# Expert stage of a two-layer decoder trunk: products of three token pairs staggered in one step, outputs brought back in 64-row products, pair-wise weights

## The reference, cut to what matters

```
g_idx = argmax(t @ w_group + b_group)              # 4 groups of experts
top_p, top_i = top_k(softmax(e_logits[g_idx]), 2)   # 2 of the 8 experts of that group
weights = g_w * top_p / sum(top_p)
y_e = (silu(x_e @ w_gate[e]) * (x_e @ w_up[e])) @ w_down[e]   # 1024 -> 256 -> 1024, for each expert e
out[token] = x[token] + sum over its 2 experts of weight * y_e
```

## Time and profile before

| | |
|---|---|
| median of 3 runs | 1148.37 us (1148.35 to 1148.47) |
| the profiled execution | 1148.85 us |
| its span, first to last instruction | 1147.0 us |
| TensorE busy | 1103.0 us, 96% |
| VectorE busy | 672.4 us, 59% |
| ScalarE busy | 372.9 us, 33% |
| GpSimd busy | 67.5 us, 6% |
| DMA queue of SyncE | 240.78 MB, 52.6% of 16 engines' span |
| mean granted TensorE clock | 0.987 |

### The profile page before, as it was taken

The page is one execution under the profiler, slowest core; times in us unless marked ns, Lnnn a source line. Parts: engine busy times, 40 slices in busy tenths (PEclk is TensorE's granted clock), DMA queues, the critical chain, the costliest instruction groups (busy, mean ns, idle before and its releaser), DMA issues.

```text
span 1147.0 us, 16734 instructions
## 1 busy us (share of the span) xinstructions
PE 1103.0 (96%) x4876; PEld 600.0 (52%) x4876; DVE 672.4 (59%) x1580; ACT 372.9 (33%) x811; POOL 67.5 (6%) x123
## 2 busy tenths in 40 slices
PE   7999999999799999999999999999997999999997
PEld 4854555556574444444457545555566544444443
DVE  4236765467685555555652477655667755555554
ACT  5226331114433333333252263210243433333332
POOL 1000000000007000000000000000000250000001
PEclk9999999999889999999999999999997999999999
DMA  9031024500319999999641300245005299999992
GB/s 351 2 109 39 1 74 147 220 1 1 151 73 406 417 421 421 423 422 422 263 157 44 103 1 1 75 147 220 1 2 220 108 404 422 421 423 422 421 422 105
DMA packets 50925, 243.20 MB, mean 212 GB/s; under 512 B 6512, under 2 KB 16784, under 8 KB 25520
## 3 DMA queue, kind: packets, MB, share of 16 engines
q1 hardware_dynamic: 50048, 240.78, 52.6%
q0 software_dynamic: 384, 1.31, 0.3%
q10 hardware_dynamic: 432, 0.38, 0.1%
HBM read 240.36 MB, written 2.10 MB: 211 GB/s over the span
## 4 chain that ended last, share of the span: by engine, by line
PE 85%; DVE 7%; ACT 2%; issue 2%; DMA 1%; DVEq 1%; ACTq 0%; POOLq 0%; SPq 0%
PE ps L2756 19%; PE ps L2300 12%; PE ps L2782 10%; PE ps L2564 9%; PE ps L2290 7%; PE ps L2717 6%; PE ps L2718 5%; PE ps L2268 5%; PE ps L2612 2%; PE ps L2383 2%; PE ps L2327 2%; DMA X<-in_x 1%; PE ps L2422 1%; PE ps L2619 1%; DVE xlo L2013 1%
## 5 line engine op out<-in xcount | busy, mean ns | idle before, releaser
L2756 PE MATMUL ps<-wgu,xw 128*64 128x512 f32 x1024 | 225.2, 592 | 0.2
L2127 DVE TENSOR_TENSOR X<-ps,X 128x512 f32<-128x512 f32 x253 | 154.5, 682 | 6.9 <-issue 6.1
L2300 PE MATMUL ps<-hT,ring 128*128 128x512 f32 x352 | 156.8, 595 | 0.0
L2756 PEld LDWEIGHTS ps<-wgu,xw 128*64 128x64 f32 x1024 | 73.5, 137 | 145.7 <-issue 144.0
L2782 PE MATMUL ps<-wdn,hhT 128*64 128x512 f32 x512 | 116.9, 598 | 0.0
L974 ACT ACTIVATE xw<-xgT 128x512 f32 (+1 forms) x132 | 81.9, 624 | 107.3 <-issue 92.9
L2564 PE MATMUL ps<-ring,yT 128*128 128x512 f32 x256 | 115.0, 596 | 0.9 <-DVE ssqY L1798 0.8
L2717 PE MATMUL ps<-yhi,Wt 128*128 128x512 f32 x256 | 106.6, 416 | 0.2
L2300 PEld LDWEIGHTS ps<-hT,ring 128*128 128x128 f32 x352 | 64.6, 190 | 69.8 <-issue 69.8
L2718 PE MATMUL ps<-ylo,Wt 128*128 128x512 f32 x256 | 100.9, 394 | 0.0
L2148 DVE SCALAR_TENSOR_TENSOR ylo<-ps,ws,yhi 128x512 fp32r<-128x512 f32 x64 | 48.1, 751 | 63.8 <-ACTq L1370 63.3
(11 more groups left out here) (364 smaller groups left out, 1344.5 us busy)
## 6 DMA issues: line engine op xcount, KB each, us to landing
wgu<-in_w_gate SPq DMA_DIRECT2D x64, 1024.0 KB, 10.3
wgu<-in_w_up SPq DMA_DIRECT2D x64, 1024.0 KB, 12.4
wdn<-in_w_down SPq DMA_DIRECT2D x64, 1024.0 KB, 12.6
ring<-in_w_in SPq DMA_DIRECT2D x8, 1024.0 KB, 6.6
ring<-in_w_mix_out SPq DMA_DIRECT2D x12, 512.0 KB, 6.3
w_kv<-in_xa_w_kv SPq DMA_DIRECT2D x4, 1024.0 KB, 8.5
ring<-in_w_in SPq DMA_DIRECT2D x2, 2048.0 KB, 15.5
ring<-in_w_in SPq DMA_DIRECT2D x2, 1536.0 KB, 14.0
```

Of the source, the lines that this page charges most:

```text
L2127: tt(xh, bank, xh, ALU.add).then_inc(mfreed((what, n)), 1)
L2300: last = mm(bank, w[:, c, c0:c0 + P], hT[:, c, :], start=c == 0, stop=c == KD - 1)
L2756: last = mm(bank[r], xw[:, c, j, 0:SLOTS], wgu[2 * parity + j][:, :, c, :], start=c == 0, stop=c == KD - 1)
```

## The change

What it does, part by part:

- **Order of TensorE's step.** A step is now: gate and up of pair p; half 0 of the bring-back of pair p-2; down of pair p-1; half 1 of the bring-back of pair p-2; flips of pair p. Bring-back of pair 14 and 15 and down of pair 15 follow the loop. ScalarE and VectorE follow the same order; `Wt` of pair p is made at the end of VectorE's step p.
- **Bring-back in 64-row products.** The slots of a pair are laid out so that partitions 0 to 63 hold the first 32 slots of both experts and partitions 64 to 127 the last 32. Lists are placed so that the first window holds tokens of tiles 0 to 2 alone and the second tokens of tiles 1 to 3 alone. A half is three rounds, each of two windows by two parts, 12 products of 64 rows where there were 8 of 128 rows (24 and 16 in a step).
- **Down in 32-column products.** To write that layout, each down product is cut in two: 16 products of 32 columns in place of 8 of 64.
- **Placement.** Two more counts come from TensorE (first and third tile of each list); `list_spans` is longer and stands after `one_hot(2)` and `low_part(2)`; a new `slot_ranks` stands before `tiles_past`; the overflow table has 24 places instead of 16.
- **Weights by pair.** Gate and up of a pair are one array in HBM, in two halves along the 1024 rows; a pair is loaded by two DMAs of 2 MB and one of 2 MB for down, in place of six of 1 MB. The first half of the next gate-up is issued when the first half of the products that read the buffer is done (`gu_half`).

```
+WINDOW = SLOTS // 2
+ROUNDS = ((2, 1), (0, 3), (1, 2))
+BACK_ORDER = (0, 3, 1, 2)
...
+                def next_gate_up(p, parity):
+                    wait_apart(sp, S["gu_half"], mdone(l, p - 2, "gu_half", 1))
+                    load_gate_up(l, p, parity, 0)
+                    multiplied(l, p - 2, ("gu",))
+                    load_gate_up(l, p, parity, 1)
...
+                next_gate_up(2, 0)
+                with sp.Fori(1, PAIRS // 2 - 1) as i:
+                    next_gate_up(2 * i + 1, 1)
+                    next_down(2 * i, 0)
+                    next_gate_up(2 * i + 2, 0)
+                    next_down(2 * i + 1, 1)
...
                 def list_spans():
-                    ts(rt[:, 4, n_lists:n_lists + NE], first_count, float(SLOTS), None, ALU.min)
-                    tt(counts, first_count, rt[:, 1, NE:2 * NE], ALU.add)
-                    tt(rank[:, 2:4], rank[:, 2:4], first_count.unsqueeze(1).to_broadcast([P, 2, NE]), ALU.add)
+                    ts(kept_0, first_tile, float(WINDOW), -float(WINDOW), ALU.is_gt, ALU.mult)
+                    stt(kept_1, third_tile, float(WINDOW), count_1, ALU.add, ALU.min)
+                    dve.drain()
+                    stt(kept_0, kept_0, float(SLOTS), count_0, ALU.add, ALU.min)
+                    dve.drain()
+                    ts(room, kept_0, -1.0, float(SLOTS), ALU.mult, ALU.add)
+                    tt(over_0, count_0, kept_0, ALU.subtract)
+                    dve.drain()
+                    tt(kept_1, kept_1, room, ALU.min)
+                    dve.drain()
+                    ts(base_1, kept_1, -1.0, float(SLOTS), ALU.mult, ALU.add)
                     dve.drain()
                     nc.vector.tensor_copy(spans, rt[:, 4, 0:3 * NE])
...
+                def slot_ranks():
+                    tt(moved, rt[:, 0].rearrange(by_half, g=HALVES, e=NE), limit, ALU.is_ge)
+                    tt(count_1, count_1, kept_1, ALU.subtract)
+                    ts(count_0, over_0, float(SLOTS), None, ALU.add)
+                    tt(start_0, start_0, room, ALU.subtract)
+                    tt(start_1, start_1, kept_1, ALU.add)
+                    dve.drain()
+                    tt(moved, moved, jump, ALU.mult)
+                    tt(rank[:, 2:4], rank[:, 2:4], base_1.unsqueeze(1).to_broadcast([P, 2, NE]), ALU.add)
+                    tt(counts, count_0, count_1, ALU.add)
+                    dve.drain()
+                    tt(rank, rank, r32(5), ALU.add)
...
+                def step_(p, parity):                       # VectorE
+                    hidden(p)
+                    added(p - 2, "comb", 0)
+                    low_parts(p - 1, 1 - parity)
+                    added(p - 2, "comb", 1)
+                    spread(parity)
...
-                step_(PAIRS - 1, 1, True)
+                added(PAIRS - 2, "comb", 0)
+                low_parts(PAIRS - 1, 1)
+                added(PAIRS - 2, "comb", 1)
                 if l < DEPTH - 1:
-                    bring_back(PAIRS - 1, "last comb", LAST_ORDER)
+                    for half in range(2):
+                        added(PAIRS - 1, "last comb", half)
...
+                def bring_back(p, what, half, parity):      # TensorE
+                    c = slice(half * 512, (half + 1) * 512)
+                    for r in range(3):
+                        if r == 2:
+                            wait_apart(pe, S["one_window"], mdone(l, p, "one_window", 2 * half + 2))
+                        for part, y in enumerate((yhi, ylo)):
+                            for window, t in enumerate(ROUNDS[r]):
+                                first, final = r < 2 and part == 0, r > 0 and part == 1
...
+                                rows = slice(window * HALF, (window + 1) * HALF)
+                                last = mm(bank, Wt[rows, parity, t * P:(t + 1) * P], y[rows, parity, c],
+                                          start=first, stop=final)
...
+                def step_(p, parity, used, used_before):
+                    gate_up(p, parity, used)
+                    pe.wait_ge(S["ylo_ready"], mdone(l, p - 2, "ylo_ready", 2))
+                    pe.wait_ge(S["Wt_ready"], mdone(l, p - 2, "Wt_ready", 1))
+                    bring_back(p - 2, "comb", 0, parity)
+                    down(p - 1, 1 - parity, used_before)
+                    bring_back(p - 2, "comb", 1, parity)
+                    hidden_turned(p)
...
+                pe.wait_ge(S["ylo_ready"], mdone(l, PAIRS - 2, "ylo_ready", 2))
+                pe.wait_ge(S["Wt_ready"], mdone(l, PAIRS - 1, "Wt_ready", 1))
+                bring_back(PAIRS - 2, "comb", 0, 0)
+                down(PAIRS - 1, 1, PAIRS // 2 - 1)
+                bring_back(PAIRS - 2, "comb", 1, 0)
```

More of the change, by code:

```diff
@@ L129, in pack_params, with gate_up_pairs, down_pairs @@
     return out
+def gate_up_pairs(gate, up):
+    shape = (DEPTH, PAIRS, 2, P, 2, KD // 2, FF)
+    both = np.stack([np.asarray(gate).reshape(shape), np.asarray(up).reshape(shape)], axis=6)
+    return np.ascontiguousarray(both.transpose(0, 1, 4, 3, 2, 5, 6, 7)).reshape(DEPTH, PAIRS, 2, P, 2, KD * FF)
+def down_pairs(down):
+    by_pair = np.asarray(down).reshape(DEPTH, PAIRS, 2, P, 2 * D).transpose(0, 1, 3, 2, 4)
+    return np.ascontiguousarray(by_pair)
 class Banks:
@@ L370, in moe_plans @@
             head.use(("sorted", half, c), (c + KD // 2) % KD)
+    for k in range(2):
+        head.use(("places", k), k)
+    head.use(("wslot",), 2)
     for b in (head, step, tail):
[L372 removed]
         b.use(("gu",), 4, frees=2)
[L374 to L384 removed]
+        b.use(("hhT",), 5)
         for h in range(2):
             b.use(("down", h), 6 + h, frees=2)
[L387 to L388 removed]
+        for half in range(2):
+            for t in (2, 1, 0, 3):
+                if b is tail:
+                    b.use(("last comb", (t, half)), BACK_BANKS[t] + (4 if half == 0 else 0))
+                else:
+                    b.use(("comb", (t, half)), BACK_BANKS[t])
     return head, step, tail
@@ L404 @@
 )
-MOE_COUNTS = dict(xw_ready=1, Wt_ready=1, silu_ready=1, hh_ready=1, hhT_ready=1, yhi_ready=2, ylo_ready=2)
+MOE_COUNTS = dict(gu_half=1, one_window=4, xw_ready=1, Wt_ready=1, silu_ready=1, hh_ready=1, hhT_ready=1, yhi_ready=2, ylo_ready=2)
 def build(nc, a, out):
@@ L1595, in positions_turned @@
                 ts(past[:, 0:7], iota[:, 1:8], float(SLOTS), None, ALU.mult)
+                for quarter in (1, 2):
+                    j, first_slot = row_place(quarter)
+                    rows = slice(quarter * WINDOW, (quarter + 1) * WINDOW)
+                    ts(slot_0[rows], slot_0[rows], float(j * SLOTS + first_slot - quarter * WINDOW), None, ALU.add)
                 ts(descending[:], iota[:, 0:NE], -1.0, 2.0 * NE, ALU.mult, ALU.add)
@@ L2108, in slot_weights @@
                     w = bank[:, 0:NE].rearrange("p (a j) -> p j a", j=2)
-                    nc.vector.tensor_copy(ws[0:HALF], w[0:HALF, 0])
-                    nc.vector.tensor_copy(ws[HALF:P], w[HALF:P, 1]).then_inc(mfreed(("wslot",)), 1)
+                    for quarter in range(4):
+                        rows = slice(quarter * WINDOW, (quarter + 1) * WINDOW)
+                        last = nc.vector.tensor_copy(ws[rows], w[rows, row_place(quarter)[0]])
+                    last.then_inc(mfreed(("wslot",)), 1)
                     signal("ws_ready")
@@ L2135, in step_, with low_parts @@
                     signal("hh_ready")
-                    if back:
-                        bring_back(p, "comb", range(8))
-                    else:
-                        ranks_shown()
-                        signal("params_free")
-                        slot_weights()
-                        dve.wait_ge(S["places_ready"], done(l, "places_ready", 2))
-                        spread(parity)
+                def low_parts(p, parity):
                     for h in range(2):
@@ L2164, in _ @@
                 one_hot(3)
+                slot_ranks()
                 tiles_past()
@@ L2170, in _ @@
                 token_weights()
-                step_(0, 0, False)
+                hidden(0)
+                ranks_shown()
+                signal("params_free")
+                slot_weights()
+                dve.wait_ge(S["places_ready"], done(l, "places_ready", 2))
+                spread(0)
+                hidden(1)
+                low_parts(0, 0)
+                spread(1)
                 with dve.Fori(0, PAIRS // 2 - 1) as i:
-                    for k in range(2):
-                        step_(2 * i + 1 + k, 1 - k, True)
+                    step_(2 * i + 2, 0)
+                    step_(2 * i + 3, 1)
                 wait_apart(dve, S["route_ready"], l + 2)
@@ L2687, in _ @@
                     for j in range(per):
-                        last = mm(bank[:, (NT + half) * NE:(NT + half + 1) * NE], ones16[:], M16[:, half * per + j, :],
-                                  start=j == 0, stop=j == per - 1)
```

(5 more changed lines are left out.)

255 lines of the change are left out of this document (126 added, 129 removed).

## The result

The changed kernel takes 1167.93 us (median of four runs, 1165.69 to 1171.45) against 1148.42 for the kernel before in the same session: ratio 1.0168, 95% interval 1.0138 to 1.0197, so 1.7% slower. The forecast was 1153 us with a range of 1142 to 1163. The sign was right and the size was not. The profiled execution of the changed kernel took 1166.91 us, its span 1165.2.

The account below looks back on a forecast made before the run. TensorE's instruction order was taken as the bound, with DMA also full. Earlier last gate-ups and later ends, -2 x 9.3 + 12.1 + 10.2 = +3.7 us, plus 1.0 for the clock, gave 1153 us; range 1142 to 1163.

Parts of the forecast that it names:

- The step: TensorE's steady step from gate-up to gate-up: 14.18 us in place of 14.58, -0.40 us.
- the loads: Weight DMAs in the expert stage: fewer, larger transfers don't matter while the loading lead stands.
- the shapes: Changes of array shape in TensorE's step: five, costing 0.88 us in place of 0.34, a loss of 0.54.
- Rival 1: TensorE's step: shape changes hidden by loading weights ahead, step 13.64 us, total 1145 us; chance 0.25.
- rival 3: Down products: four 32-column products keep less than the pace of two; 1180 to 1260 us; chance 0.06.
- Rival 4: Bring-back: 64-row float32r pairs don't run together, +89 us, 1240 us; chance 0.02.
- The head: Ahead of the first step: added VectorE placement operations, uncovered, start gate-up 0 2.7 us later.
- Rival 2: Before the first step: the delay is 1.5 us, not 2.7, and the clock holds; 1149.7 us; chance 0.20.
- the failed step: First steps of the stage: TensorE's work alone puts gate-up 1 at 349.8 us and gate-up 2 at 360.8.
- Hidden: ScalarE and VectorE work within a step: VectorE's last ends some 12.7 us after gate-up, within 14.2.
- E + 24.3: Next layer's TensorE start, 24.3 us after the bring-back behind the last gate-up begins; +12.1 us over before.
- Rival 5: Clock falls in both layers and waits in bring-back rounds aren't hidden: +12 us, 1161 us; chance 0.12.

Follow-up runs that it names:

- e8: Kernel before with only the pair-wise weights (2 MB transfers in place of six of 1 MB): 1148.80 us, ratio 0.9995.
- e10: Kernel before with ten more small VectorE operations in the head of the stage, results unread: 1154.96 us, ratio 1.0050.
- e1: Changed kernel with ScalarE reading the next pair's six span registers before it waits for gate-up: 1160.92 us, ratio 1.0100.
- e9: Changed kernel with unread filling products ahead of gate-up 0 and ahead of the wait for pair 15's table: 1185.30 us, ratio 1.0318.
- e2: Changed kernel with TensorE waiting separately for the tables of pairs 14 and 15 after the loop: 1162.96 us, ratio 1.0121.
- e5: Changed kernel with early span registers, down 15 before outputs of 14, separate table waits, VectorE's overflow reads after its additions: 1154.80 us, ratio 1.0040.
- e6: Changed kernel with outputs brought back in 16 products of 128 rows instead of 24 of 64: 1186.40 us, ratio 1.0326.
- two-line form: Changed kernel with bring-back of pair p-1 around flips and down of pair p, span registers read early: 1180.37 us, ratio 1.0260.

## Why the prediction was right in sign and wrong in size

**The step, the loads and the shapes: right.** 14.21 for 14.18. Rival 1 (shape changes hidden) falls by the joints of 0.33; rival 3 falls by 3.64 us for the narrow down products. By the Trainium skill (TensorE: Matmul & The Clock Gate, Part 3: Packing small matmuls), three column tiles give a speedup of 2.38; in this trace four 32-column products take no longer than two of 64 (3.64 and 3.65 us for a pair), so the measurement decides. Rival 4 falls by the pairs at 0.23. The loads I called harmless: e8 shows it for the kernel before, and in the changed kernel TensorE is busy for all of 540 to 554 us, the last steps of layer 0, so it waits for no load there.

**The head: right.** +3.0 for my +2.7, and operations of that length make it by themselves (e10). Rival 2, which wanted half of it, falls.

**Ahead of the steady steps: the failed step.** "After: 338.15 + 14.9 - 3.5 (down 0 comes later) + 0.2 = 349.8 for gate-up 1; gate-up, down 0 and flips (7.0 + 3.6 + 0.4) to 360.8 for gate-up 2" counts TensorE's own work alone. I had written "ScalarE copies four windows before `yhi`" and "Hidden" for the step, where bring-back, down products and flips, 7 us, lie between two gate-ups. Ahead of gate-up 1 and 2 there are no outputs to bring back yet: 4.6 us of TensorE's work lie between gate-up 0 and 1 and 4.0 between 1 and 2. The way there, from the end of gate-up over silu and 5.1 us of reads and copies, is 5.7 to 6.4 us. Measured: 1.0 and 2.3 us of wait in layer 0, 1.3 and 2.3 in layer 1, and in layer 0 gate-up 1 took 8.78 us and not 7.09, at a granted clock of 0.79 in 352 to 360 us. Sum 5.2 and 3.7, two thirds of the error, of which 1.7 the clock's. So the term that was put at nothing is ScalarE's way from gate-up to the next windows. e1 takes it away and gives the forecast's distances to 0.2 us.

**The end: right in its waits, short in the clock.** The idle of 3.94 us was forecast as 3.8, and the restart at E + 24.3 came at E + 26.5. The 2.2 us between are the low clock behind the idle (2.1 by the products themselves and by e9; in layer 1 1.5 of 1.6). I had seen that in the earlier trace rows, priced it at 1.7, and then taken 1.0 for both layers, since I held it for uncertain whether it would fall. It fell in both, and cost 3.6 us together; this term was too small by 2.6. Rival 5 had the clock in both layers and 1161 us; its other half, waits in the rounds, did not happen.

**What e2 corrects.** I named the wait on the wrong table as the reason of the idle. It was the nearest one only: with it gone, VectorE held TensorE back 2.5 us at the same place. My own list of VectorE's work had it: half 1 of pair 13 is added by E + 9.4, and a bank is wanted at E + 7.4.

**The sign.** That the change costs time was forecast from the head and the deferred end, and both are there. But the forecast was +0.4%, with a chance of 0.45 on the same or faster; nearly half of the measured 1.7% (8.9 of 19 us) comes from the term that I had at nothing, so the sign is not much to the credit of the sum.

**What is open.** Why the clock fell behind some waits of 1 to 2 us and not behind others (e1 and e5 have the same first waits, e5 has low stretches in the prologue of layer 0, e1 none; e9 and the changed kernel differ so at gate-up 1 of layer 1) wasn't settled. e5's two groups speak for a clock that falls in some executions of one and the same kernel and not in others, but only one execution of each kernel was profiled. Nor was a two-line form without my wait at its end tried.

## What to carry to other kernels

Deeper staggering is paid twice: where the pipeline fills, the work that hid a helper engine's chain isn't there yet, and where it drains there is nothing left to hide the last items. So take every "hidden in the step" and check it again for the first two and the last two steps, each with the distance it has there. A gain of 0.37 us in each of the fourteen full steps is 5 us a layer; an unhidden 3 us of small VectorE operations in the head and one wait of 4 us with a low clock behind it were more than that. And when a wait is removed, look up who is next: here another engine kept 2.5 of the 3.9 us.

## What the runs showed of the hardware

- Four 32-column products side by side cost what two 64-column ones do: 3.64 and 3.65 us for a pair's down products.
- Two 64-column streams overlap almost fully: sixteen products in alternating halves 7.09 us, in one half 13.95 (e9).
- A change of tile shape cost 0.14 to 0.21 us of TensorE's time in every direction seen; behind gate-up's 64 columns the first product took 0.33 or 0.34 us whether 64 rows or 128 followed (changed kernel and e6).
- A register load between ScalarE's copies costs about 0.4 us of its time, an estimate from 2.5 us of "issue" with six of them in the chain of 5.1 us in the changed kernel, against 0.4 where they were read ahead (e1).
- The granted clock fell to 0.5 (1.2 GHz) behind TensorE's waits of 3.9 us in both layers of the changed kernel (0.50 in 572 to 574 and in 1146 to 1148 us), and 2.1 us of the end of layer 0 came from that alone. Behind waits of 2.3 (its gate-up 2, layer 0) and 2.47 us (e2) it stayed at 1.00, and behind 1.0 (its gate-up 1, layer 0) it fell: the length of the last wait alone doesn't say whether it falls.
